# A two-layer decoder trunk: expert sums held in four PSUM banks, and half a weight chunk loaded ahead

## What is computed

```
x = x + even_mixer(rmsnorm(x))        # layer 0: gated recurrence and sparse attention
x = x + hier_moe(rmsnorm(x))
x = x + odd_mixer(rmsnorm(x))         # layer 1: sliding-window attention
x = x + hier_moe(rmsnorm(x))

hier_moe(h):                          # 256 tokens of 1024, all float32
    choose one of 4 groups, then the best 2 of its 8 experts for every token
    y[token] += weight * (silu(h @ w_gate[e]) * (h @ w_up[e])) @ w_down[e]
```

## Time and profile before

| | |
|---|---|
| median of 3 runs | 1170.49 us (1166.68 to 1170.76) |
| profiled execution | 1170.16 us, of which the span of the trace is 1168.4 us |
| mean granted TensorE clock | 0.911 of full speed |
| busy | PE 76%, PEld 54%, DVE 29%, ACT 16%, POOL 2% |
| read from main memory | 440.01 MB, 377 GB/s over the span |
| chain that ended last | DMA 53%, PE 39%, DVE 3%, issue 2% |

### The profile page before, as it was taken

One profiled execution on the slowest core, in us unless ns is written; L12 is line 12 of the kernel. 1 busy time (PEld: TensorE's weight loads), 2 busy tenths in 40 slices (PEclk: granted clock), 3 DMA queues, 4 the chain that ended last, 5 costly groups with the idle time before them and its releaser, 6 DMA issues.

```text
span 1168.4 us, 28535 instructions
## 1 busy us (share of the span) xinstructions
PE 883.7 (76%) x12710; PEld 626.4 (54%) x12710; DVE 336.1 (29%) x996; ACT 189.2 (16%) x496; POOL 28.6 (2%) x32
## 2 busy tenths in 40 slices
PE   7999998787575757575778999887675666665765
PEld 6766657575454535353546556665544454544454
DVE  3476735132020202020204764322120212121201
ACT  4223522110000000000003443011000000000000
POOL 2121000000000000000000000000000000000000
PEclk9999999998797989888889999899988888889889
DMA  9955337899999999999999846999999999999996
GB/s 377 429 186 218 144 144 290 369 422 426 429 429 427 428 430 429 427 429 430 428 424 427 354 196 225 407 384 427 430 430 425 430 430 427 427 430 429 427 427 284
DMA packets 32683, 441.93 MB, mean 378 GB/s; under 512 B 3696, under 2 KB 4848, under 8 KB 6128
## 3 DMA queue, kind: packets, MB, share of 16 engines
q1 hardware_dynamic: 32336, 440.92, 90.2%
q10 hardware_dynamic: 288, 0.15, 0.0%
HBM read 440.01 MB, written 1.05 MB: 377 GB/s over the span
## 4 chain that ended last, share of the span: by engine, by line
DMA 53%; PE 39%; DVE 3%; issue 2%; ACT 1%; SPq 1%; DVEq 0%; ACTq 0%
DMA side<-weights 42%; DMA ring<-weights 11%; PE PS L485 11%; PE PS L929 7%; PE PS L916 5%; PE PS L643 1%; PE PS L543 1%; PE PS L808 1%; PE PS L495 1%; PE PS L939 1%; PE PS L532 1%; PE PS L570 1%; PE PS L1045 1%; SPq L325 1%; PE PS L552 1%
## 5 line engine op out<-in xcount | busy, mean ns | idle before, releaser
L916 PE MATMUL PS<-ring,probT 128*32 128x128 f32 x4480 | 150.5, 294 | 61.8 <-DMA ring<-weights 56.7
L916 PEld LDWEIGHTS PS<-ring,probT 128*32 128x32 f32 x4480 | 134.2, 119 | 78.3 <-DMA ring<-weights 66.2
L916 PE MATMUL PS<-side,probT 128*32 128x128 f32 x2688 | 106.2, 322 | 70.1 <-DMA side<-weights 67.6
L916 PEld LDWEIGHTS PS<-side,probT 128*32 128x32 f32 x2688 | 92.6, 131 | 89.4 <-DMA side<-weights 84.2
L485 PE MATMUL PS<-ring,side 128*128 128x512 f32 (+1 forms) x320 | 134.9, 573 | 0.4 <-DMA ring<-weights 0.4
L1484 DVE TENSOR_TENSOR scr<-scr,PS 128x128 f32<-128x128 f32 x64 | 18.4, 287 | 400.0 <-ACT scr L1388 336.6
L1985 DVE COPY probT<-PS 32x256 f32<-32x256 f32 x112 | 47.5, 424 | 173.1 <-PE PS L929 172.3
L929 PE MATMUL PS<-side,scr 128*32 128x256 f32 x896 | 71.6, 470 | 28.8 <-DMA side<-weights 24.0
L485 PEld LDWEIGHTS PS<-ring,side 128*128 128x128 f32 x320 | 59.1, 190 | 61.6 <-issue 59.9
L929 PE MATMUL PS<-ring,scr 128*32 128x256 f32 x896 | 67.4, 448 | 19.7 <-DMA ring<-weights 10.6
L1392 ACT ACTIVATE probT<-PS 32x256 f32<-32x256 f32 x112 | 41.8, 373 | 232.8 <-PE PS L929 232.1
(11 more groups left out here) (278 smaller groups left out, 844.9 us busy)
## 6 DMA issues: line engine op xcount, KB each, us to landing
ring<-weights SPq DMA_DIRECT2D x127, 2048.0 KB, 34.6
side<-weights SPq DMA_DIRECT2D x80, 2048.0 KB, 27.2
ring<-weights SPq DMA_DIRECT2D x4, 512.0 KB, 8.7
xn<-xT_in SPq DMA_DIRECT2D x2, 512.0 KB, 5.5
x<-x_in SPq DMA_DIRECT2D x2, 512.0 KB, 8.7
out<-x SPq DMA_DIRECT2D x4, 256.0 KB, 2.6
TB<-table SPq DMA_DIRECT2D x1, 781.5 KB, 16.4
SM<-small SPq DMA_DIRECT2D x1, 732.0 KB, 17.6
```

The lines of the kernel that those rows point to most:

```text
L916: mm = pe.matmul(PS[f * CAP:(f + 1) * CAP, b, up * P:(up + 1) * P], gatherT[:, k, tok], w[:, k, f * P:(f + 1) * P], start=(k == 0), stop=( ...
```

## The change

1. Four PSUM banks, 6, 4, 7 and 5, keep the sum of all experts' outputs from the first quad to the last. A quad ends with eight products of 256 columns (L962 of the changed kernel) that add to them; VectorE's four additions to `x` in each quad but the last go. The outputs of down move from banks 4 and 5 to banks 0 and 1, which the gather also uses.
2. `xn` isn't made. The tokens are gathered from `x`, by picks that are multiplied by `rs`. So VectorE makes the one-hot picks in `pickw`, then `pick` as `pickw` times `rs`, and then `pickw` times the expert's weight in place.
3. The 8 KB of `xn` take the first half of chunk 11 of a layer's first quad. SyncE issues this half between two loads of the mixer: in layer 0 behind chunk 5 and a wait for `cat_turned`, in layer 1 behind chunk 4 and a wait for the last `head_ssq` (`xn` serves the mixers until then). The second half is loaded where the whole chunk was.

```
+        OUT = (6, 4, 7, 5)
+        spare = xn[:, :, :].rearrange("p a n -> p (a n)")
+        HALF = CW // 2
...
+                def second_half_of_first():
+                    sp.wait_ge(chunk_done, done + 6 + QC * at)
+                    sp.dma_start(buffer(TWICE)[:, HALF:CW], weights[base + QC - 1, :, HALF:CW]
+                                 ).then_inc(w_landed[TWICE], 16)
...
-                last_of(at + 1)
+                second_half_of_first()
...
+            def first_half(base):
+                sp.dma_start(spare, weights[base + QC - 1, :, 0:HALF]).then_inc(half_landed, 16)
...
+                if free is cat_ready:
+                    sp.wait_ge(cat_turned, TT)
+                    first_half(MOE0)
...
+                if j == 4:
+                    sp.wait_ge(head_ssq, len(groups))
+                    first_half(MOE1)
...
-                    mm = pe.matmul(PS[:, half, k * P:(k + 1) * P], xn[:, t, d * P:(d + 1) * P], pick[:, t, :],
+                    mm = pe.matmul(PS[:, half, k * P:(k + 1) * P], x[:, t, d * P:(d + 1) * P], pick[:, t, :],
...
-                for n in range(4):
-                    t, half = n // 2, n % 2
-                    if n >= 2:
-                        pe.wait_ge(m_acc[0], 2 * i + n - 1)
-                    pe.matmul(PS[:, 6 + n % 2, :], pickT[:, t * P:(t + 1) * P],
-                              yq[:, half * 512:(half + 1) * 512], start=True, stop=True).then_inc(m_comb, 1)
+                for t in range(TT):
+                    for q in range(4):
+                        pe.matmul(PS[:, OUT[q], t * 256:(t + 1) * 256], pickT[:, t * P:(t + 1) * P],
+                                  yq[:, q * 256:(q + 1) * 256], start=(first and t == 0), stop=False,
+                                  skip_group_check=True)
...
-                act.wait_ge(rs_last, layer + 1)
-                act.activation(xn[:, 1, :], x[:, 1, :], ACT.Copy, scale=s("rs")[:, 1:2]).then_inc(xn_ready, 1)
...
-                else:
-                    dve.tensor_scalar(xn[:, t, :], x[:, t, :], s("rs")[:, t:t + 1], None,
-                                      ALU.mult).then_inc(xn_ready, 1)
...
-                tt(pk, last(rk, CAP), iota, ALU.is_equal).then_inc(m_onehot, 1)
-                dve.wait_ge(m_onehot, n)
+                tt(pk, last(rk, CAP), iota, ALU.is_equal).then_inc(m_raw, 1)
+                dve.wait_ge(m_raw, n)
+                tt(pick[:, :, :], pickw[:, :, :], last(s("rs"), P), ALU.mult).then_inc(m_onehot, 1)
...
+                return dve.tensor_scalar(pick[:, t, :], pickw[:, t, :], s("rs")[:, t:t + 1], None, ALU.mult)
...
-                for n in range(4):
-                    dve.wait_ge(m_comb, 4 * i + n + 1)
-                    xs = x[:, n // 2, (n % 2) * 512:(n % 2 + 1) * 512]
-                    tt(xs, xs, PS[:, 6 + n % 2, :], ALU.add).then_inc(m_acc[n // 2], 1)
```

More of the change, by code:

```diff
@@ L223, in build @@
         dve_step, act_step, pool_step = sem("dve_step"), sem("act_step"), sem("pool_step")
-        x_ready, ssq_ready, rs_ready, xn_ready = sem("x_ready"), sem("ssq_ready"), sem("rs_ready"), sem("xn_ready")
+        x_ready, ssq_ready, rs_ready = sem("x_ready"), sem("ssq_ready"), sem("rs_ready")
         rs_refined = sem("rs_refined")
@@ L870, in router @@
                           skip_group_check=True).then_inc(ranked, 1)
-                pe.wait_ge(xn_ready, TT * (layer + 1))
             def gather(i, layer):
@@ L879, in gather @@
                             d = 4 * half + k
-                            mm = pe.matmul(PS[:, half, k * P:(k + 1) * P], xn[:, t, d * P:(d + 1) * P],
+                            mm = pe.matmul(PS[:, half, k * P:(k + 1) * P], x[:, t, d * P:(d + 1) * P],
                                            pick[:, t, :], start=(t == 0), stop=(t == TT - 1))
@@ L925, in quad @@
                     w = moe_landed(layer, i, 3 * e + 2).rearrange("p (f n) -> p f n", f=4)
+                    early = first and e == QE - 1
+                    if early:
+                        pe.wait_ge(half_landed, 16 * (layer + 1))
+                        w0 = spare.rearrange("p (f n) -> p f n", f=2)
                     pe.wait_ge(m_hidT, QE * i + e + 1)
@@ L928, in quad @@
                         for q in range(4):
[L929 removed]
+                            mm = pe.matmul(PS[q * CAP:(q + 1) * CAP, e % 2, 0:256],
                                            hidT[:, e % 2, f * CAP:(f + 1) * CAP],
[L931 removed]
+                                           (w0 if early and f < 2 else w)[:, f, q * 256:(q + 1) * 256],
+                                           start=(f == 0), stop=(f == 3))
                     mm.then_inc(chunk_done, 1)
                 pe.wait_ge(m_y, 2 * QE * i + 2 * QE)
[L935 to L940 removed]
+                for t in range(TT):
[3 more added lines that the diff above has]
+                                  skip_group_check=True)
             def turn_picks(i):
@@ L959, in combine @@
                 pe.wait_ge(m_y, 2 * QE * i + 2 * e + 2)
-                if e == 0:
-                    for t in range(TT):
-                        pe.wait_ge(m_acc[t], 2 * i)
                 for t in range(TT):
@@ L1150, in norm @@
                     for half in range(2):
-                        act.wait_ge(m_acc[half], iters * 2)
+                        act.wait_ge(m_acc[half], 2)
                 else:
@@ L1906, in router @@
                 add_quarter(layer, 1, first_chunk, iters)
-                first_picks(layer, 0).then_inc(first_picked, 1)
+                first_picks(layer, 0, None).then_inc(first_picked, 1)
                 evacuate_last(layer, 1)
@@ L1926, in router @@
                 dve.wait_ge(chosen, 2 * layer + 2)
-                first_picks(layer, 1).then_inc(m_onehot, 1)
-                dve.wait_ge(m_onehot, build)
+                first_picks(layer, 1, build).then_inc(m_onehot, 1)
                 tt(rt[:, 4, :, :], rt[:, 0, :, :], rt[:, 3, :, :], ALU.subtract)
@@ L1935, in router, with first_picks @@
                 link(dve.tensor_scalar(s("w1"), s("e2"), 1.0, None, ALU.add))
-            def first_picks(layer, t):
+            def first_picks(layer, t, build):
                 dve.wait_ge(ranked, 2 * layer + t + 1)
@@ L1941, in first_picks @@
                                               rt[:, 0, t, :], ALU.add, ALU.mult))
-                return tt(pick[:, t, :].rearrange("p (e c) -> p e c", e=QE), last(rank[:, t, 0:QE], CAP),
-                          mid(tb("iota"), QE), ALU.is_equal)
+                raw = tt(pickw[:, t, :].rearrange("p (e c) -> p e c", e=QE), last(rank[:, t, 0:QE], CAP),
+                         mid(tb("iota"), QE), ALU.is_equal)
+                if t == 0:
+                    link(raw)
+                else:
+                    raw.then_inc(m_raw, 1)
+                    dve.wait_ge(m_raw, build)
+                return dve.tensor_scalar(pick[:, t, :], pickw[:, t, :], s("rs")[:, t:t + 1], None, ALU.mult)
             def weights_and_count(layer, build):
@@ L2002, in last_quad @@
                         for q in range(4):
-                            dve.wait_ge(m_comb, 4 * i + q + 1)
+                            dve.wait_ge(m_comb, 4 * layer + q + 1)
                             xs = x[:, :, q * 256:(q + 1) * 256]
```

42 lines of the change are left out of this document (19 added, 23 removed).

## The result

| | before | after |
|---|---|---|
| median, runs | 1170.18 us, 6 | 1173.72 us, 6 |
| lowest to highest | 1166.68 to 1170.77 | 1172.74 to 1175.36 |
| ratio, 95% interval | | 1.0033 [1.0021, 1.0044] |

The changed kernel is 3.5 us slower, inside the 0.5% that count as no difference; 1171.6 was forecast, 1.5 us above before. With this many runs the interval shows a loss.

A forecast was written before the change was run, and what follows sets the result against it. TensorE's end of each first quad was taken to release fixed-length saturated streams. Profiled 1170.16 us plus 1.48 for the picks, all other terms 0, gave 1171.6 us, range 1165.0 to 1177.0.

The forecast's parts named there:

- The bound: Expert stages: saturated streams of fixed length start at the releases, when TensorE ends each layer's first quad; TensorE sets that moment.
- The half chunk, value 0: First quads: loading half of chunk 11 early only lengthens idle transfers by 2.45 us; 0 gained, bounds 0 and 4.9 us.
- the stream binds the first quad after all: Rival, first quads: half chunks count in full, VectorE's terms are hidden; 4.9 us gained, 1165.3 us; chance 0.10.
- The copies of `x` and the sums, 0: Mixer-to-router copies were hidden; PSUM sums stand behind the release or in saturated stretches: both bring 0.
- The picks, 1.48 us: Router and first quad, both layers: VectorE's scalings on the path, 2 x (0.32 + 0.42) us, ends 0.9 and 1.6.
- 1170.16 plus 1.48: Whole kernel: the profiled execution's time plus the picks' cost gives 1171.6 us.
- The loads of chunk 5: Sign of being right: second quads' chunk 5 loads come about 0.7 and 1.5 us later, at the same TensorE clock and holes.
- The rival without holes: First quads: TensorE's holes of 1.92, 0.78, 1.22 us and low-clock down products go; 1165.1 us; chance 0.07.
- The rival of the lower clock: First quads: longer wait ahead of first transpose drops TensorE's clock; four more down groups at 1.69 us, 1178.4 us; chance 0.09.
- other waits there stay under 1 us: First quads: argument against the lower-clock rival, that TensorE's waits other than the one ahead of the first transpose stay short.
- low-clock stretches in other places: Sign of being wrong: such TensorE stretches move a release by more than the two VectorE terms.

The follow-up runs named there:

- the old order: SyncE's loads as before; the new order issues the second quad's chunks 6, 7, 8 ahead of chunk 5: before 1165.02 us, changed kernel 1159.83 us.
- the kernel with the whole chunk: Changed kernel with chunk 11 of the first quads loaded whole at its old place, nothing into `xn`: 1173.74 us, 1.0028 to before.
- the sums alone: Kernel before with only part 1, the sums in four PSUM banks; `xn`, picks and loads as they were: 1170.78 us, 1.0004.
- the pair of late picks: Second quad's picks made behind the first expert's copy of the transpose, in the changed kernel 1166.87 us, in the kernel before 1166.99 us.
- the waits at the start: Kernel before with eighty waits that are met at once, ahead of TensorE's first product: 1173.90 us, 1.0037.
- the forty hidden ones: Kernel before with forty more TensorE wait instructions in layer 0's last quad, where TensorE waits for data: 1171.60 us, 1.0016.
- the dose run: Changed kernel with chunk 11 loaded whole and three more of each new VectorE scaling, written to places nobody reads: 1177.22 us, 1.0075.

## Why the prediction was right, and where its size was off

No measurable difference was forecast, and the time lies well inside the range; the added time is 3.5 us where 1.5 was forecast.

**The bound.** Right. Both saturated parts are equal to 0.1 us before and after, and the kernels with the old order have 396.6 to 397.3 us in the second.

**The half chunk, value 0.** Right, by the kernel with the whole chunk (1173.74 against 1173.72). Its down product still waits 0.48 us for VectorE's copy. The rival "the stream binds the first quad after all" falls for this order, and its 4.9 us are what the half is worth in the other.

**The copies of `x` and the sums, 0.** Right within what the runs can tell: 1.0004 with the sums alone. The picks then carry most of the loss, 2.8 of some 3.5 us.

**The picks, 1.48 us.** The place is right, the direct term somewhat smaller: 0.23 and 0.32 us in the router where 0.32 was taken, 0.34 and 0.25 ahead of the transpose where 0.42 was. That is 1.14 us of 3.5. The step that fell short is "1170.16 plus 1.48": it held TensorE's clock and its holes as they are. The loads of chunk 5, forecast 0.7 and 1.5 us later, came 0.3 and 2.6 us later. Two things were left out, and how they share the rest isn't settled.

The first is the clock at the gather, which the account of the picks looked at only for its length. The second part of the gather now starts behind a wait of 1.0 us. There are seven profiles of kernels with scaled picks, with two first quads each. In 6 of these 14 the gather and the group behind it ran partly at the lower clock and lost 1.6 us, once 2.9. In the 12 first quads of the six kernels without scaled picks, with waits of 0.69 and 0.78 us, it never happened there. Spread over the 14 it is 1.6 us for an execution; with the 1.14 that makes 2.7, near the 2.8 that came with the scaled picks. This is an estimate from single executions, and no run changes the clock alone. The changed kernel's own profile, its fastest execution, has no such fall, so it can't show this part.

The second is the holes, which lie elsewhere in layer 1 because the change takes and adds TensorE instructions in every quad. Of the profiled 2.3 us in layer 1, this is the larger part: 0.84 us at the hole and 0.79 at the last group of gate and up. The kernel with the sums alone, without any scaling, lost 2.4 us there. The medians don't agree on its price. The kernel with the sums alone is only 0.5 us above before; the waits at the start cost 4.2 us, of which 4.1 passed ahead of the first product; the forty hidden ones cost 1.9. All three moved the holes, and their intervals overlap. And since the sums already move the holes, they don't explain the 2.8 us between the kernel with the sums alone and the one with the scaled picks. In layer 0, where few instructions have gone by, the holes lie almost where they were (behind 103 and not 102 products).

Against a large part for either speaks the pair of late picks: both are still in the changed kernel there, and it is 0.6 us slower than the other, with 2 us of doubt. So it is shown that the scaled picks cost time on the path and that 1.14 us is their direct length. What makes up the other 2.4 us stays open.

**The rival without holes.** It didn't come about: the holes are 1.54, 1.05 and 2.06 us, where they were 1.92, 0.78 and 1.22.

The prediction cited the Trainium skill, page "Runtime: NRT & Kernel Launch", section "Instruction fetch mechanics", for a rule by which such holes wouldn't be there to be won. Of that page two figures fit: blocks of 16 KiB with 256 instructions each, by the row of the instruction queue in the profile (0.75 MB in 46 packets, 16 KB each) and by the 254 to 256 instructions from hole to hole. "Mostly hidden" doesn't fit in the first quads: the holes there are 0.2 to 2.8 us. They lie where the transfer engines are full, and that the fetch stands behind the data there is argued, not shown.

**The rival of the lower clock.** Its mechanism is real, though not in the number that would have made 1178 us. Behind the wait it named, ahead of the first transpose, the fall was there before the change: the down product took 2.90 and 3.62 us, and 2.97 and 3.44 after. With the group behind it, that is 7.4 us both times before, 7.4 and 7.1 after, and 5.6 in all six first quads with late picks, where the wait is 0.96 to 1.06 us. In the dose run it is 8.3 us behind a wait of 2.81 and 7.4 behind one of 3.02, so a longer wait made it worse at most once. Where the change did add falls is at the gather, a wait that this rival didn't look at: it said that "other waits there stay under 1 us", and this one went from 0.78 and 0.69 to 1.01 us; the prediction's own sign of being wrong, "low-clock stretches in other places", names them. The length of the wait alone doesn't decide: behind 1.01 us the gather kept its clock in 7 of 12 cases. The clock also falls behind holes: the down group behind the changed kernel's hole at 754.92 us takes 3.64 us, which is one more reason why a border's place has a price.

## What to carry to other kernels

Before a load is made smaller or earlier, look whether the transfer engines run dry ahead of the point where the next long stream starts; if so, find the load at the head of the queue that waits, and put those behind it whose buffers are free first. An instruction on a second engine between a product and the one that waits for it costs its own length, and at some waits clock as well: move what nobody needs yet behind the hand-over. Moving instructions alone changed this kernel by up to 2 us (0.2%), and two executions of one program can differ by as much on the way to the same product. A difference of this size needs medians, and an experiment that moves instructions and changes nothing else.

## What the runs showed of the hardware

- In the first quads, where dense small products run, TensorE stands idle 0.2 to 2.8 us at places 127 or 128 products apart, some 256 instructions; 40 instructions more moved each hole by 20 products. A border can also pass without a hole when the clock is low: in the kernel before, at a clock of 0.53 just ahead of it, the group took 4.04 us in one piece.
- With a wait of 1.0 us in place of 0.7 to 0.8 ahead of 16 products, these products and the group behind them lost 1.6 to 2.9 us to the lower clock in 5 of 12 cases; with the shorter wait in none of 12. In the one worked out above the granted clock is 0.50 over 4 us.
- A wait for a semaphore whose value has long been reached isn't free on TensorE: 80 waits, of which the profile counts 40 instructions, delayed the first product by 4.08 us, 0.10 us for each pair; 57 pairs ahead of an expert go with 4.2 to 5.3 us of idle time.
- One blocked load in SyncE's in-order queue left the transfer engines at 190 and 281 GB/s over 8 us, with three free buffers behind it.
- A `tensor_scalar` over 128 float32 columns took 0.29 us, as long as the comparison ahead of it.
